# Output projection that also forms and stores the operands of the first FFN half

## The reference

```
x = x + concat([o_a, o_b, o_c]) @ w_out           # output projection and residual
h = rms_norm(x, norm_ffn)                         # x * rsqrt(mean(x^2)) * gain
up = causal_dwconv(h @ ffn_w_up, conv_w, conv_b)  # 1024 -> 5632, width 3
u_val, u_gate = split(up)
x = x + (gelu(u_gate) * u_val) @ ffn_w_down       # 2816 -> 1024
```

## Time and profile before

| | us |
|---|---|
| runs | 2995.87, 2995.99, 2999.19; median 2995.99 |
| profiled execution, its own time | 2997.87 |
| its span | 2996.0 |
| output projection, first load to last `rstd` | 1327.9 to 1532.8 |
| FFN head, from there to PE without a stop | to 1603.9 |
| up part of half 0 (PE busy for 396.00 of the 396 us from 1604) | 1604 to 2013 |
| down part of half 0 | 2013.6 to 2267.1 |
| up part of half 1 | 2267 to 2711 |
| down part of half 1 | 2711.5 to 2963.4 |

### The profile page before, as it was taken

One profiled execution on the slowest core, in us unless ns is written; L12 is line 12 of the kernel. 1 busy time (PEld: TensorE's weight loads), 2 busy tenths in 40 slices (PEclk: granted clock), 3 DMA queues, 4 the chain that ended last, 5 costly groups with the idle time before them and its releaser, 6 DMA issues. The chain is left out here.

```text
span 2996.0 us, 33843 instructions
## 1 busy us (share of the span) xinstructions
PE 2590.8 (86%) x12320; PEld 2107.9 (70%) x12320; DVE 1615.9 (54%) x1936; ACT 1070.7 (36%) x1683; POOL 776.8 (26%) x615
## 2 busy tenths in 40 slices
PE   7999999599985775139948999999998999998996
PEld 5888888289984553027836888877786888887874
DVE  7211111555554544963258777765456787774335
ACT  5000000056675332422124444433524444442332
POOL 3110100322320200811245333313203443330003
PEclk9999999899997555669978999999999999999998
DMA  4211211400003003245331222227542322224463
GB/s 148 92 70 70 74 70 63 195 21 28 27 33 120 26 25 124 95 165 174 113 114 57 85 85 85 85 74 260 183 148 74 120 104 80 85 78 153 143 221 109
DMA packets 117319, 304.99 MB, mean 102 GB/s; under 512 B 16640, under 2 KB 29712, under 8 KB 108752
## 3 DMA queue, kind: packets, MB, share of 16 engines
q1 hardware_dynamic: 117200, 303.46, 28.8%
HBM read 217.14 MB, written 86.28 MB: 101 GB/s over the span
## 5 line engine op out<-in xcount | busy, mean ns | idle before, releaser
L1831 PE MATMUL ff_bank<-ff_b_hi,ff_ring 128*128 128x512 f32 x1232 | 485.2, 394 | 64.4 <-DVE ff_ring L2371 46.5
L1833 PE MATMUL ff_bank<-ff_b_hi,ff_ring 128*128 128x512 f32 x1232 | 483.3, 392 | 0.0
L1832 PE MATMUL ff_bank<-ff_b_lo,ff_ring 128*128 128x512 f32 x1232 | 483.2, 392 | 0.0
L1831 PEld LDWEIGHTS ff_bank<-ff_b_hi,ff_ring 128*128 128x128 f32 x1232 | 233.8, 190 | 118.3 <-issue 66.1
L43 PE MATMUL ip_bank<-ip_x_hi,ip_w_hi 128*128 128x512 f32 x736 | 291.1, 396 | 20.1 <-DVE ip_x_lo L255 17.0
L1831 PE MATMUL ff_bank<-ff_a_hi,ff_w_hi 128*128 128x512 f32 x704 | 278.9, 396 | 27.3 <-DVE ff_a_lo L2423 27.3
L44 PE MATMUL ip_bank<-ip_x_lo,ip_w_hi 128*128 128x512 f32 x736 | 289.0, 393 | 0.0
L45 PE MATMUL ip_bank<-ip_x_hi,ip_w_lo 128*128 128x512 f32 x736 | 288.8, 392 | 0.0
L1832 PE MATMUL ff_bank<-ff_a_lo,ff_w_hi 128*128 128x512 f32 x704 | 277.4, 394 | 0.0
L1833 PE MATMUL ff_bank<-ff_a_hi,ff_w_lo 128*128 128x512 f32 x704 | 277.1, 394 | 0.0
L2409 DVE SCALAR_TENSOR_TENSOR ff_y<-ff_u,ff_conv_all,ff_y 128x1024 f32<-128x1024 f32 x176 | 240.9, 1369 | 62.8 <-ACT ff_y L2253 59.6
(11 more groups left out here) (246 smaller groups left out, 4961.1 us busy)
## 6 DMA issues: line engine op xcount, KB each, us to landing
ff_raw<-in_slabs SPq DMA_DIRECT2D x44, 1024.0 KB, 4.7
ff_a_raw<-a_t SPq DMA_DIRECT2D x88, 512.0 KB, 3.9
proj_t<-ip_staged SPq DMA_DIRECT2D x92, 256.0 KB, 2.3
a_t<-ff_y SPq DMA_DIRECT2D x44, 512.0 KB, 2.6
ff_w_raw<-in_w_down SPq DMA_DIRECT2D x88, 256.0 KB, 2.7
ip_w_raw<-in_w_in SPq DMA_DIRECT2D x23, 512.0 KB, 3.4
o_scratch<-at_o_sb SPq DMA_DIRECT2D x48, 198.0 KB, 1.9
cb_rows<-o_scratch SPq DMA_DIRECT2D x24, 396.0 KB, 4.1
```

The source lines that it names most:

```text
L1831: pe.matmul(out, w_hi, x_hi, start=first, stop=False, skip_group_check=resumed)
L1832: pe.matmul(out, w_hi, x_lo, start=False, stop=False, skip_group_check=resumed)
L1833: return pe.matmul(out, w_lo, x_hi, start=False, stop=last, skip_group_check=resumed)
```

## The change

In words, part by part:

- **Output projection, x.** A third slot `x_third` lies where `w_raw` was and takes block 2, loaded early. Block 3 goes into slot 0, once the operands in it have been stored. Mix loads of block b+2 now stand right behind the store of block b, or, for block 3, behind the stores of block 1, of B00 and of B10.
- **Output projection, operands.** After blocks 0 and 1 are done and stored, DVE normalises them in place (`norm`, 16 instructions, after m = 3 and 4 of the next block) and forms T1, T3, T2, T4 in place (`combine`, 16 instructions, after m = 4 to 7 of block 2). SP stores the seven operands to a new buffer `h_t`, 1 MB each.
- **Output projection, order.** `sum_squares` after m = 0, `invert` after m = 2, `root` in the middle of the `high` copies.
- **FFN head.** Seven loads of `h_t` in place of the four pieces; no `norm_b` and no `combine_b` in the first half.
- **Down part.** `x2d` loaded at n = 14; pieces at n = 3, 6, 9, 12; slabs of the second half at n = 33, 36; `norm_b` one per step, n = 6 to 21; `high_b` from n = 26 and `low_b` from n = 28; store of x3 and next load of `x2d` 4 steps later. The first pass's squares go two per step, n = 23 to 26. At the end of half 0, `keep(1, 0, 0)` stands after six squares of eight.

```
@@ output_projection, SP @@
             def load_x(b):
-                if b >= 2:
-                    sp.wait_ge(stored[b % 2], 16 * (b // 2))
-                    sp.wait_ge(square_ready, KT * (b - 1))
+                if b == 2:
+                    sp.wait_ge(w_ready, OUT_SLABS)
+                if b == 3:
+                    sp.wait_ge(h_stored[T1], 16)
+                    sp.wait_ge(h_stored[T4], 16)
...
+            load_mix(1)
+            load_x(2)
             for b in range(BLOCKS):
...
                 sp.wait_ge(added, KT * (b + 1))
+                sp.dma_start(x2_t[:, :, blk(b)], xs[b]).then_inc(stored, 16)
+                if b == 0:
+                    load_mix(2)
+                if b == 1:
+                    store_h(B00, x[:, 0, 0:KH, :], normed, KH)
+                    store_h(B10, x[:, 0, KH:, :], normed, KT)
+                    load_mix(3)
+                    store_h(B11, x[:, 1, KH:, :], normed, 2 * KT)
+                    store_h(T1, x[:, 0, 0:KH, :], t_ready, KH)
+                    store_h(T3, x[:, 1, 0:KH, :], t_ready, 2 * KH)
+                    store_h(T2, x[:, 1, KH:, :], t_ready, 3 * KH)
+                    store_h(T4, x[:, 0, KH:, :], t_ready, 4 * KH)
+                    load_x(3)
@@ output_projection, DVE @@
+            def norm(b, k):
...
+                dve.scalar_tensor_tensor(out=xs[b][:, k, :], in0=xs[b][:, k, :], scalar=gain[:, k:k + 1], in1=rstd[:, blk(b)],
...
+            def combine(o, k):
...
+                    ins = dve.tensor_tensor(first[:, k, :], second[:, k, :], first[:, k, :], ALU.subtract)
...
-                    if b and m == KT // 2:
+                    if b and m == 2:
                         invert(b - 1)
+                    if b in (1, 2) and m in (3, 4):
+                        for k in range(KH * (m - 3), KH * (m - 2)):
+                            norm(b - 1, k)
+                    if b == 2 and m in (4, 5, 6, 7):
+                        for k in range(KH):
+                            combine((T1, T3, T2, T4)[m - 4], k)
@@ conv_ffn, SP @@
+            load_h(B00)
+            load_slab(0, 0)
+            for o in (T1, T2, B10):
+                load_h(o)
+            load_slab(0, 1)
+            for o in (T3, T4, B11):
+                load_h(o)
+            sp.dma_start(conv_all[:, :, :, :], conv).then_inc(consts_in, 16)
             sp.dma_start(gain[:, :, :], gains).then_inc(gain_in, 16)
...
-                    if n == 2:
+                    if half == 0 and n in (3, 6, 9, 12):
+                        load_piece(1, n // 3 - 1)
+                    if n == 14:
                         load_x2d(half, 0)
...
@@ conv_ffn, ACT @@
-                    if n == PAIRS + 1:
-                        square(half, 0)
+                    if PAIRS + 1 <= n < PAIRS + 5:
+                        square(half, 0, range(2 * (n - PAIRS - 1), 2 * (n - PAIRS)))
...
+                    square(0, 1, range(6))
+                    keep(1, 0, 0)
+                    square(0, 1, range(6, 8))
+                    high_w(1, 8)
```

More of the change, by code:

```diff
@@ L1609, with output_projection @@
 TAPS = 3
-def output_projection(nc, mix_t, x_t, w_slabs, rstd, x2_t):
+PASSES = 2
+OC = KT // PASSES
+KH = KT // 2
+FFN_ORIGIN = 24704
+B00, T1, T2, B10, T3, T4, B11 = range(7)
+def output_projection(nc, mix_t, x_t, w_slabs, norm_gain, rstd, x2_t, h_t, origin):
     with ExitStack() as ctx:
@@ L1655, in output_projection @@
         rstd_ready = sem("rstd_ready")
-        stored = [sem(f"stored{i}") for i in range(2)]
+        stored = sem("stored")
+        gain_in = sem("gain_in")
+        normed = sem("normed")
+        t_ready = sem("t_ready")
+        h_stored = [sem(f"h_stored{o}") for o in range(7)]
         block = ctx.enter_context(nc.Block())
+        xs = [x[:, 0, :, :], x[:, 1, :, :], x_third[:, :, :], x[:, 0, :, :]]
         def blk(b):
@@ L1720, in square @@
                         act.wait_ge(summed, n - 1)
-                    act.activation(squares[:, n % 2, :], x[:, b % 2, k, :], ACT.Square).then_inc(square_ready, 1)
+                    act.activation(squares[:, n % 2, :], xs[b][:, k, :], ACT.Square).then_inc(square_ready, 1)
             def root(b):
@@ L1727, in _ @@
             weights_high(0)
-            high(0)
+            high(0, range(KT))
             for n in range(1, OUT_SLABS):
@@ L1848, in sem @@
             return used[-1]
-        B00, T1, T2, B10, T3, T4, B11 = range(7)
         RING = 11
@@ L1905, in conv_ffn @@
         halo_zeroed = sem("halo_zeroed")
+        h_in = [sem(f"h_in{o}") for o in range(7)]
         x2_in = [sem(f"x2_in{i}") for i in range(4)]
@@ L2268, in high_step, with square @@
                 act.activation(a_hi[n % 2][:, :], a_raw[n % 2][:, :], ACT.Copy).then_inc(d_hi_ready, 1)
-            def square(half, p):
-                for i in range(8):
+            def square(half, p, tiles):
+                for i in tiles:
                     n = 16 * half + 8 * p + i
@@ L2363, in low_b @@
                 dve.wait_ge(b_hi_ready, 28 * half + 4 * HI_AT[o] + k + 1)
-                reader = {B00: T1, T1: T2, T2: T4, B10: T4, T3: T3, T4: T4, B11: T3}[o]
-                dve.wait_ge(t_ready, 16 * half + 4 * T_AT[reader] + k + 1)
+                if half:
+                    reader = {B00: T1, T1: T2, T2: T4, B10: T4, T3: T3, T4: T4, B11: T3}[o]
+                    dve.wait_ge(t_ready, 4 * T_AT[reader] + k + 1)
                 dve.tensor_tensor(b_lo[:, o, k, :], b_raw[:, o, k, :], b_hi[:, o, k, :].bitcast(F32), ALU.subtract).then_inc(b_lo_ready, 1)
@@ L2492, in _ @@
                         drain(half, 0)
-                    if half == 0 and 5 <= n < 13:
-                        for i in range(2 * (n - 5), 2 * (n - 5) + 2):
-                            norm_b(1, i)
-                    if half == 0 and n >= 24:
-                        for i in range(2 * (n - 24), min(2 * (n - 24) + 2, 28)):
+                    if half == 0 and 6 <= n < PAIRS:
+                        norm_b(n - 6)
+                    if half == 0 and n >= 28:
+                        for i in range(2 * (n - 28), min(2 * (n - 28) + 2, 28)):
                             low_b(1, i)
```

149 lines of the change are left out of this document (77 added, 72 removed).

## The result

The changed kernel takes 2956.84 us (median of four runs, 2953.11 to 2959.09) against 2995.99 for the kernel before (four runs beside it, 2995.87 to 2999.19): ratio 0.9866, 95% interval 0.9848 to 0.9883. The forecast was 2955 in a range of 2947 to 2968. The profiled execution took 2957.88, its span 2956.1 (before 2997.87 and 2996.0), with PE busy 87% and the mean granted clock at 0.912 (before 0.906).

A forecast was written before the change was run, and what follows sets the result against it. The prediction took PE (86% busy) as the bound, so only its stops and the low clock behind them counted. Terms 23.4 - 1.0 + 15.5 + 1.8 + 1.2 = 40.9 us off 2997.87 gave 2957.0, as median 2955, range 2947 to 2968.

The forecast's parts named there:

- Head: FFN head: operands loaded ready-made, A11 starts at 1580.5 instead of 1603.92, with about 11 us idle before S2; gain 23.4 us.
- the first MB is there at 1542.5: FFN head: landing time of the first 1 MB load, from which PE was to start about 1546.2.
- Output projection: Output projection: DVE gains 16 norms and 16 subtractions; 3 us lost use up the margin, PE stalls 1; loss 1.0 us.
- What can come through is block 3's x: Output projection: only block 3's x, loaded after T4's store, could delay PE, at product 28; margin two to three us.
- I take 3 us lost: Output projection, block 2: DVE loses 3 us beside POOL, which is the margin, leaving 1 us of stall.
- rival 1: Output projection, block 2: the shared port makes DVE 7 us late, PE stops 5 instead of 1; 2959 us, chance 0.14.
- Squares: Down part: two squares per step remove the step 24 stops and low clock, 6.55 + 2.3 and 4.39 + 2.3; gain 15.5 us.
- Loads: Down part: later x2d removes half 0's step 3 stop (0.8) and brings step 2 of half 1 sooner (1.0).
- Turn: Turn to half 1: S2 starts earlier, but only the 1.23 that S3's copy waited for PE goes; gain 1.2 us.
- The second: FFN head rival: slower loads or a later clock rise give 5.4 to 8 us less; 2960 to 2963, chance 0.11.
- The third: Down part rival: DVE's drain at n = 22, or n = 26, stops PE instead, 8.9 not gained; 2964, chance 0.08.
- the slower case: Output projection rival: at 2.0 us per DVE operation in block 2, PE stops 48 us; about 3002, chance 0.02.

The follow-up runs named there:

- e11: Changed kernel with the operand buffer `h_t` laid out as `x2_t`, 2 KB rows and 64 KB between partitions: 2963.32 us.
- e3: Changed kernel with ACT's head copies for S2, S3 and A11 moved up behind the fourth, fifth and seventh operand: 2948.76 us.
- e4: Changed kernel with block 3's last three splits done together at m = 5 of block 2, ahead of T3, T2 and T4's subtractions: 2949.29 us.
- e2: Changed kernel with the first pass's eight squares again in one go at n = 23, in both halves: 2969.02 us.
- e10: Changed kernel with the second half's pieces loaded at n = 3 to 6 and normalised two per step at n = 5 to 12: 2953.93 us.
- e7: Changed kernel with the down part's loads (x2d and the four norm pieces) back at steps 2 to 6, squares still spread: 2961.35 us.
- e1: Changed kernel with everything of the down part and turn put back as before, leaving only output projection and head changed: 2975.74 us.
- e5: Changed kernel with each stored and loaded row of `h_t` 2 KB instead of 8 KB, a gap behind every row: 2959.06 us.
- e9: Changed kernel with the copy for S2 of the second half again behind all eight squares: 2959.64 us.
- e12: Changed kernel with e3, e4 and e10 together, first two bank moves on DVE behind S4's weight split, and slab 0's last sum on DVE: 2947.92 us.

## Why the prediction was right, and where it was not

**Sign and size.** Forecast 40.9, measured 39.9 in the profiles, of which -2.9 is scatter ahead of the change. The term sizes were less good than the sum: the head gave 5.4 us more than forecast, output projection 3.0 less, the first down part with the turn 1.8 less and the second 1.3 more, and the start scattered by 2.9. That the sum comes within 1 us (and the median within 2) is luck; that it lies in the range is not.

**Head: 23.4 forecast, 28.8 measured.** Order and mechanism were as described: one early start of PE (9.9 us after the FFN's first load, forecast 12.3) and one long stop before S2 (9.96, forecast about 11), with the copy behind all seven operands as its releaser. Mis-sized was the step "the first MB is there at 1542.5": it took the first load's 8.3 us over from a differently laid out tensor. B00 came 3.4 us sooner, of which the layout accounts for 2.5 (e11); the rest of that is open. The loads behind it came at 429 instead of 405 GB/s. S2 starts 28.3 us after the first load (forecast 32.9). From S2 to A11 it took 13.06, near the 13.7 taken over. Moving the copy for S2 as well would have given 4.3 us more (e3).

**Output projection: loss 1.0 forecast, 4.0 measured.** Two steps failed. The first is "What can come through is block 3's x". It is not late; PE's wait in block 3 is for the last split of its mix (e4), 3.51 us, and the clock is low for a spell behind it (0.72 over 1484 to 1490). The prediction had DVE's queue in block 2 in hand and asked only what came last on it, not what stood in the middle with a consumer of its own. The second is "I take 3 us lost" (beside POOL). The groups beside POOL's totals lost 5.8 us ahead of that split and 1.1 behind it, 6.9 in all, which is the 7 that the prediction had worked out first and that its rival 1 stands on: right in the delay, wrong in the place where PE would meet it.

Either is enough to explain the stop. By the timeline the last split would have ended 5.8 us sooner without the loss (an estimate), and 3.51 us would have been enough; and with the order of e4 the stop goes although the norms and subtractions there lose as much (6.11, 3.47, 4.08 and 3.55 for the same groups). No run takes POOL away, so the first half of this is argued, not shown.

The 4.0 itself is one profile against one: the same code gives 198.6 to 202.3, so the loss is 2.6 to 6.3. The long ones have a low clock behind an early stop in block 0 (over 28 to 60 us from the first product it is 0.90 or 0.91 in the four profiles of 201.5 and more, 1.00 in the six up to 199.9), and the kernel before has 0.95 there, so the loss is rather above 4.0 than below.

**Squares: 15.5 forecast.** Half 1 right in mechanism, 6.8 to 8.2 where 6.7 stood. Half 0 was credited wholly to the squares; e2 gives them 2.0 beside the changed kernel and 3.4 beside e10, since there they share the stop with the edits beside them. The spread norms took 1.4 back (e10), a cost that the prediction had put at nothing. The stretch gained 9.1 of 10.85.

**Loads: 1.8 forecast, 5.3 by e7** (3.9 to 6.5), when taken out of the changed kernel. Against the kernel before little of it can be seen. The 0.79 stop is gone, but counted from the 0.78 stop at the end of the up part, step 3 of half 0 starts at 32.8 in the changed kernel (31.2 to 33.0 with the same code) and 32.9 before, and at 33.3 in e1 and e7, which have the old loads. In half 1 it starts at 31.3 in the changed kernel (31.1 to 33.3 with the same code) and 33.3 before, 33.9 and 34.1 in e1 and e7. And the 1.0 at step 2 of half 1, which fits the forecast to a tenth, is not the loads': e1 and e7 have it too (24.1), and e5, with the new loads, does not (25.2).

**Turn: 1.2 forecast, 1.2 measured** (1.0 to 2.2), for another reason: clock, not idle (e9). The agreement is luck.

**Rivals.** The second had the head as the doubtful term, on the wrong side. The third's place (steps 22 and 23) had a stop of 0.77 and cost 1.4 (e10). Block 2's operand chain, the slower case, showed 1.5 us per operation in its worst group (5.99 / 4) and 0.79 on average ((1488.3 - 1453.5 - 3.3) / 40) where the forecast needed 2.0.

## What to carry to other kernels

When work is added to an engine's queue, look at every instruction behind it in that queue and ask who waits for that one: here the first consumer to be hurt was not the one at the end of the new work. A loss beside another engine adds up along a queue that never rests. A buffer between two stages is worth laying out for its reader, each tile in one piece (3.9 us here, e11). Where a stop is removed, check whether idle time goes or only moves; a moved stop can still gain if it lowers the clock once instead of twice.

## What the runs showed of the hardware

- A POOL addition of 128x512 took 10.10 us in the changed kernel, 10.70 in the kernel before and 10.72 in e3, each time beside an unbroken row of DVE subtractions from two SBUF tiles, which kept their 0.6 us each; it ends 1.1 to 1.2 us behind the row's last. In other places DVE is slowed beside POOL (5.75 for 2.49 in e12; in the changed kernel 5.99 for 2.73 in the norms). The Trainium skill, SBUF — State Buffer, section "SBUF: two separate sides", has the loser wait for the whole instruction that holds the ports; here POOL's one instruction lasted over more than ten of DVE's, which that sentence does not lead one to expect.
- Issuing loads of 1 MB costs SP 1.63 us for three where each partition's data is one piece of 8 KB, 2.90 where it is four rows of 2 KB (e5), 3.48 in the layout of `x2_t` (e11).
